# Neighbourhood attention over column blocks: 256 of the 512 grid keys for each tile of queries, keys written group by group

## What is computed

```python
NA_HEADS, HEAD_DIM, NA_WIN_R, NA_WIN_C, GRID_W = 4, 64, 8, 16, 64     # the grid has 8 rows, so a window has all of them
col_start = np.clip(cols - NA_WIN_C // 2, 0, GRID_W - NA_WIN_C)
col_idx = col_start[:, None] + np.arange(NA_WIN_C)
def row_block(r):
    rs = jnp.clip(r - NA_WIN_R // 2, 0, rows - wr)                    # always 0
    k_w = lax.dynamic_slice_in_dim(kg, rs, wr, axis=1)[:, :, col_idx]
    bias = rpb[:, dr][:, :, dc].transpose(0, 2, 1, 3)                 # by distance in rows and in columns
    s_loc = jnp.einsum('bchd,brcjhd->bhcrj', q_r, k_w) * NA_SCALE + bias
    s_ctx = jnp.einsum('bchd,bkhd->bhck', q_r, k_ctx) * NA_SCALE
    p = jax.nn.softmax(jnp.concatenate([s_loc, s_ctx]), axis=-1)
    return einsum(p_loc, v_w) + einsum(p_ctx, v_ctx)
```

## Time and profile before

| | us |
|---|---|
| median of 3 runs | 2218.65 (2218.54 to 2220.48) |
| the profiled execution: its own time | 2219.67 |
| its span in the trace | 2217.9 |
| busy: PE | 2083.6 (94%) |
| DVE | 1200.8 (54%) |
| ACT | 750.8 (34%) |
| POOL | 644.7 (29%) |

### The profile page before, as it was taken

The page is one execution under the profiler, slowest core; times in us unless marked ns, Lnnn a source line. Parts: engine busy times, 40 slices in busy tenths (PEclk is TensorE's granted clock), DMA queues, the critical chain, the costliest instruction groups (busy, mean ns, idle before and its releaser), DMA issues.

```text
span 2217.9 us, 30035 instructions
## 1 busy us (share of the span) xinstructions
PE 2083.6 (94%) x11738; PEld 1720.0 (78%) x11738; DVE 1200.8 (54%) x2143; ACT 750.8 (34%) x1221; POOL 644.7 (29%) x820
## 2 busy tenths in 40 slices
PE   7888999989989999999999998889998979999999
PEld 4777788866668888888888877778866657888887
DVE  7467524477884776177537566663368864212111
ACT  4333323456663211111111233423266643222222
POOL 1210301220002333333333430141221014555555
PEclk9999999999999999999999999999899999999999
DMA  7301431110002233233323310021110002333223
GB/s 290 105 17 34 142 107 67 39 48 10 10 10 67 76 124 124 77 114 124 105 95 114 96 52 18 20 69 39 39 48 20 10 10 77 99 100 95 95 95 105
DMA packets 76242, 165.58 MB, mean 75 GB/s; under 512 B 5192, under 2 KB 46664, under 8 KB 75088
## 3 DMA queue, kind: packets, MB, share of 16 engines
q1 hardware_dynamic: 75728, 163.28, 22.0%
q10 hardware_dynamic: 384, 0.47, 0.1%
HBM read 161.63 MB, written 2.10 MB: 74 GB/s over the span
## 4 chain that ended last, share of the span: by engine, by line
PE 79%; DVE 11%; ACT 4%; issue 4%; PEld 1%; POOL 1%; DMA 0%; PEldq 0%; DVEq 0%; SPq 0%; ACTq 0%; POOLq 0%
PE psum L1099 22%; PE psum L1100 21%; PE psum L1101 21%; PE psum L1698 1%; DVE naptlo L2107 1%; PE psum L1150 1%; PE psum L1728 1%; PE psum L1338 1%; POOL wlo L541 1%; PE psum L1467 1%; PE psum L1453 1%; PE psum L1404 1%; PE psum L1191 1%; PE psum L1223 1%; PE psum L1405 1%
## 5 line engine op out<-in xcount | busy, mean ns | idle before, releaser
L541 POOL TENSOR_TENSOR wlo<-raw,whi 128x256 fp32r<-128x256 f32 x816 | 644.5, 821 | 1564.9 <-ACT whi L566 1564.9
L1099 PE MATMUL psum<-hhi,whi 128*128 128x512 f32 (+1 forms) x1640 | 588.4, 359 | 16.8 <-DVEq L1901 8.6
L1100 PE MATMUL psum<-hlo,whi 128*128 128x512 f32 (+1 forms) x1640 | 578.9, 353 | 0.0
L1101 PE MATMUL psum<-hhi,wlo 128*128 128x512 f32 (+1 forms) x1640 | 578.2, 353 | 0.0
L566 ACT ACTIVATE whi<-raw 128x1024 fp32r<-128x1024 f32 x204 | 215.7, 1059 | 876.7 <-PE psum L1101 870.6
L1099 PEld LDWEIGHTS psum<-hhi,whi 128*128 128x128 f32 x1640 | 312.6, 191 | 73.1 <-issue 18.8
L1101 PEld LDWEIGHTS psum<-hhi,wlo 128*128 128x128 f32 x1640 | 312.2, 190 | 42.8
L1100 PEld LDWEIGHTS psum<-hlo,whi 128*128 128x128 f32 x1640 | 312.8, 191 | 40.2 <-issue 0.2
L2540 DVE TENSOR_TENSOR ffuf<-ffsa,psum 128x768 f32<-128x768 f32 (+1 forms) x44 | 36.1, 821 | 312.6 <-ACT ffsa L1049 305.9
L2525 DVE SCALAR_TENSOR_TENSOR ffmacc<-wm,csil,ffmacc 128x256 f32<-128x256 f32 x336 | 188.5, 602 | 10.4 <-DVE ffmacc L2525 5.3
L1099 PE MATMUL psum<-uhi,whi 128*128 128x512 f32 (+1 forms) x528 | 188.4, 357 | 3.7 <-DVE ulo L2544 2.1
(11 more groups left out here) (331 smaller groups left out, 3392.5 us busy)
## 6 DMA issues: line engine op xcount, KB each, us to landing
raw<-w_stream SPq DMA_DIRECT2D x204, 512.0 KB, 3.7
wm<-w_mod SPq DMA_DIRECT2D x80, 512.0 KB, 4.0
wm<-w_mod SPq DMA_DIRECT2D x8, 1024.0 KB, 12.6
xres<-x_t SPq DMA_DIRECT2D x8, 384.0 KB, 6.4
out<-xres SPq DMA_DIRECT2D x8, 256.0 KB, 2.2
consts<-c_f SPq DMA_DIRECT2D x1, 353.0 KB, 3.1
narpb<-rpb ACTq DMA_DIRECT2D x2, 120.0 KB
mlmask<-c_gate ACTq DMA_DIRECT2D x2, 108.0 KB
```

The source lines that it names most:

```text
L541: nc.gpsimd.tensor_tensor(wlo[:, q % 2, c:c + UW // 4], raw[:, q % RAW, c:c + UW // 4], whi[:, q % 2, c:c + UW // 4], ALU.subtract).then_i ...
L1099: mm(dst, ah, bh, start=first, stop=False)
L1100: mm(dst, ah, bl, start=False, stop=False)
L1101: return mm(dst, al, bh, start=False, stop=last)
```

## The change

- **Fewer keys.** The grid is cut into four query tiles of 16 columns by 8 rows (`NA_QC`) and eight key groups of 8 columns. A tile needs four neighbouring groups (`NA_G0`): 256 keys. Grid steps have 512 keys in place of 768, scores fit one PSUM bank of three, transposes go to banks 3 and 4 in turn.
- **Layout.** `key_order` writes the keys group by group, so that the 256 keys of a tile are one contiguous run; `query_order` writes the queries tile by tile. The values come out feature-major (grid 512 and context 256 columns moving), ACT copies them in group order to `navt`, PE transposes them (nine tiles, `NA_VAT`, three of them halfway between the others), then `navhi` and `navlo` as before.
- **Bias.** Three `na_bias` quads for each layer in place of 16 groups: each 32 matmuls of 32 output partitions by 128 columns, four side by side. `bias_out` copies them to `nag`; `bias_windows` makes three masked windows for each head (`nabias`), with masks that a new DMA on ACT's queue brings.
- **Softmax.** Bias, negation and minimum are one operation over 512 columns, context included (against a zero table). One exponential. The inverse row sum is applied by ACT (`scale_of`, in place), so `nadg`, the matmul with ones and the multiplication in `o_of` go.
- **Order.** Both heads of a pair alternate (a). On PE: turn(n), scores(n+2), half of the values. On DVE: max(n+1), inverse(n), `o_of`(n-5), `lo_of`(n-1). On ACT: exponential(n), copy(n-1), scale(n). Steps are as many as before: 12 for a pair in layer 0 (4 context, 8 grid), 8 in layer 1.

```diff
@@ att_plan, layout
+        def query_order(x, e):
+            return x[:, CTX_LEN:].rearrange("p (t m c e) -> p e m t c", t=4, m=4, c=16, e=2)[:, e]
+        def key_order(x):
+            return x[:, CTX_LEN:].rearrange("p (g r c) -> p r g c", g=8, c=8)
@@ PE: na_bias, values
-                for half in (0, 64):
-                    ins = mm(bias_bank(l, g)[half:half + 64, 0:240], band[:, 60 - 4 * g:60 - 4 * g + 64],
-                             NA["rb"][:, :], start=True, stop=True)
+                for g in range(4):
+                    at = 1 + 2 * (44 - 4 * (4 * q + g))
+                    for odd in range(2):
+                        for m in range(4):
+                            r = NA_WIN_R - 1 - 2 * m - odd
+                            ins = mm(bias_bank(l, q)[32 * m:32 * m + 32, P * g:P * g + P], band[:, at - odd:at - odd + 32],
+                                     rows[:, :, r:r + NA_WIN_R], start=odd == 0, stop=odd == 1)
-                    for t in range(TT):
-                        dst = bank(t)[:, 0:256]
-                        mm(dst, hhi[:, k, P * t:P * t + P], wh[:, c:c + 256], start=k == 0, stop=False)
...
+                    for f in range(2):
+                        a = slice(c + P * f, c + P * f + P)
+                        mm3(bank(f), wh[:, a], wl[:, a], hhi[:, k, CTX_LEN:], hlo[:, k, CTX_LEN:], k == 0, k == KT - 1)
...
+                    for n in {3: (0, 1), 4: (2,), 6: (3, 4)}.get(g, ()):
+                        turn_values(n)
@@ PE: att_pe
+                    if s >= 3:
+                        pe.wait_ge(s_nmx, s - 2)
...
-                for n in range(N + 3):
-                    if n < N:
-                        scores(*steps[n])
-                    if 1 <= n < N + 1:
-                        turn(*steps[n - 1])
...
+                scores(*steps[0])
+                scores(*steps[1])
+                for n in range(N + 2):
+                    if n < N:
+                        turn(*steps[n])
+                    if n + 2 < N:
+                        scores(*steps[n + 2])
+                    if n >= 2:
+                        values(n % 2, *steps[n - 1 - n % 2])
@@ ACT: att_act
+                def scale_of(s, b, kind, t, a):
+                    act.wait_ge(s_rs, s + 1)
+                    A(p, p, ACT.Copy, scale=stat[:, s % 2, 6:7]).then_inc(s_sc, 1)
...
-                    if n:
-                        hi_of(*steps[n - 1])
-                    exp_of(*st)
+                    exp_of(*st)
+                    if n:
+                        hi_of(*steps[n - 1])
+                    scale_of(*st)
@@ DVE: att_dve
+                        V.tensor_tensor_reduce(two(NA["s2"][:, s % 2, :]), two(bank(s % 3)), NA["bias"][:, 0:w + 1:w, :],
+                                               -1.0, -NEG, ALU.add, ALU.min, lowest).then_inc(s_nmx, 1)
...
+                    V.reciprocal(stat[:, s % 2, 6:7], stat[:, s % 2, 4:5]).then_inc(s_rs, 1)
...
+                max_of(*steps[0])
+                for n in range(N + 5):
+                    if n + 1 < N:
+                        max_of(*steps[n + 1])
                     if n < N:
-                        max_of(*steps[n])
...
+                        rs_of(*steps[n])
+                    if n >= 5:
+                        o_of(*steps[n - 5])
                     if 1 <= n < N + 1:
-                        rs_of(*steps[n - 1])
                         lo_of(*steps[n - 1])
```

More of the change, by code:

```diff
@@ L25 @@
 NEG = -1.0e30
+NA_X = 3
+NA_QC, NA_G0, NA_VAR = (0, 16, 32, 48), (0, 1, 3, 4), (0, 1, 1, 2)
+NA_VX = ((2, 3), (6, 7), (7, 8), (4, 5))
+NA_TILES = TT + NA_X
+NA_VAT = tuple(P * t for t in range(TT)) + tuple(CTX_LEN + 64 + P * t for t in range(NA_X))
+BIAS_QUADS = 3
+MASKS_AT = 3 * P + 122 + 2
 UW = 1024
@@ L283, in att_blocks @@
         def att_blocks(l):
-            return ([0] if l < DEPTH - 1 else []) + [1, 2]
+            return ([("c", 0), ("c", 1)] if l < DEPTH - 1 else []) + [("x", t) for t in range(4)]
         def att_plan():
@@ L717, in hi_of @@
-                def hi_of(s, b, blk, qt, nk):
+                    A(NA["p"][:, s % 3, 0:nk], NA["s2"][:, s % 2, 0:nk], ACT.Exp, bias=st[:, 0:1], scale=-1.0,
+                      accum_out=st[:, 4:5]).then_inc(s_exp, 1)
+                def scale_of(s, b, kind, t, a):
+                    nk = 256 if kind == "c" else 512
+                    act.wait_ge(s_rs, s + 1)
+                    p = NA["p"][:, s % 3, 0:nk]
+                    A(p, p, ACT.Copy, scale=stat[:, s % 2, 6:7]).then_inc(s_sc, 1)
@@ new lines, in att_pe, with scores, turn, values @@
+            def att_pe(l, pr):
+                steps = PLAN[l, pr]
+                def scores(s, b, kind, t, a):
+                    if s >= 3:
+                        pe.wait_ge(s_nmx, s - 2)
+                    dst = bank(s % 3)
+                    qh, ql = (queries(NA[x][:, a, :], kind, t) for x in ("qhi", "qlo"))
+                    ins = mm3(dst[:, 0:CTX_LEN], qh, ql, NA["khi"][:, 0:CTX_LEN], NA["klo"][:, 0:CTX_LEN], True, True)
+                    if kind == "x":
+                        at = CTX_LEN + 64 * NA_G0[t]
+                        kh, kl = (NA[x][:, at:at + 256] for x in ("khi", "klo"))
+                        ins = mm3(dst[:, CTX_LEN:512], qh, ql, kh, kl, True, True)
+                    ins.then_inc(s_ps, 1)
+                def turn(s, b, kind, t, a):
+                    pe.wait_ge(s_sc, s + 1)
+                    if s >= 2:
+                        pe.wait_ge(pt_lo, s - 1)
+                    for k in range(2 if kind == "c" else 4):
+                        ins = nc.tensor.transpose(bank(3 + s % 2)[:, P * k:P * k + P], NA["p"][:, s % 3, P * k:P * k + P], ident)
+                    ins.then_inc(t_ps, 1)
+                def values(part, s, b, kind, t, a):
+                    tiles = (0, 1) if kind == "c" else (0, 1) + NA_VX[t]
+                    half = len(tiles) // 2
@@ L2023, in query_split @@
             def query_split(l, full, a):
-                q0 = 0 if full else CTX_LEN
-                seq(split(NA["qhi"][:, a, q0:], NA["qlo"][:, a, q0:], NA["t"][:, q0:]))
+                hi_, lo_, t = NA["qhi"][:, a, :], NA["qlo"][:, a, :], NA["t"]
+                parts = [(query_order(hi_, e), query_order(lo_, e), grid_order(t, e)) for e in range(2)]
+                if full:
+                    parts.append((hi_[:, 0:CTX_LEN], lo_[:, 0:CTX_LEN], t[:, 0:CTX_LEN]))
+                for h, _, x in parts:
+                    ins = V.tensor_copy(h, x)
+                seq(ins)
+                for h, w, x in parts:
+                    ins = V.tensor_tensor(w, x, h, ALU.subtract)
+                seq(ins)
             def na_key(l, pr):
@@ L2054, in na_inputs @@
-                    if l:
-                        bias_out(l, g)
+                    if l and g in (0, 2, 5):
+                        for x in range(2):
+                            bias_out(l, (0, 2, 5).index(g), x)
+                    for n in {3: (0, 1), 4: (2,), 6: (3, 4)}.get(g, ()):
+                        values_lo(l, n)
+                    if g == 7:
+                        bias_windows(l)
                     if g == 14:
@@ L2128, in att_dve @@
                         lo_of(*steps[n - 1])
-                    if n >= 4 and steps[n - 4][4] == 1:
-                        o_of(*steps[n - 4])
+                dve.wait_ge(o_lo, steps[-1][0] + 1)
             def ml_dve(l, full):
```

349 lines of the change are left out of this document (174 added, 175 removed).

## The result

| | before | changed |
|---|---|---|
| median of five runs each, side by side | 2218.65 us (2217.44 to 2221.18) | 2208.66 us (2206.89 to 2212.73) |
| ratio, 95% interval | | 0.995 (0.9935 to 0.9965) |
| profiled execution, span | 2217.9 us | 2205.6 us |
| mean granted TensorE clock | 0.982 | 0.968 |

The changed kernel is faster by 10.0 us (0.5%), where 22.6 were forecast; 2208.66 lies outside the range of 2186 to 2207.

What follows compares the result with a forecast made beforehand. DVE paced the old attention steps; afterwards a wait through ACT, PE and DVE would. Terms -1.6, -19.7, +1.4, -4.1, +0.95 sum to -23.1 us: forecast 2196 us, range 2186 to 2207 (8 in 10).

Steps and rivals of the forecast that it cites:

- The clock: Rival: PE in the attentions at 1.2 GHz instead of 2.4 all through, +53 us, 2249 us; chance 5%.
- the loop: Attention grid steps: scaling, transposes, scores, minimum, inverse and four hand-overs follow in a circle, 3.06 us per step.
- the prediction's own layout: Attention pair's instructions in written order, each starting when engine and operands are ready: 36.8 us layer 0, 28.5 layer 1.
- The attentions otherwise: Four attentions, shortfall included: 37.3 us each in layer 0, 28.9 each in layer 1; 19.7 us gained.
- Start and layer 0: Start up to the first attention: bias groups leave PE's chain, DVE's sums of squares end 0.9 us later; -1.6 us net.
- weights that come late for the new, earlier time: Start, layer 0: late weight DMAs could take from the gain there; no size given.
- The quads: Layer 1 bias: 32 matmuls of 128 columns, four side by side, 2.0 us a quad, 6.0 for three.
- the third rival: Bias quads bound for each matmul, 4.0 us a quad: +6 us in layer 1, +3 in the start, 2205; chance 12%.
- Values and bias of layer 1: Layer 1, values to attention: cheaper bias, added transposes, a wait gone, keys' split +0.35; -4.1 us.
- the stretch with the splits: Between a layer's attentions (pair 1): query and key splits in more pieces, +1.4 us in layer 0, +0.95 in layer 1.
- The second rival: Strided outputs and splits cost DVE twice: 0.6 us per output piece, pairs 39.2 and 31.0 us, 2208; chance 9%.
- first rival: Attention grid steps set by engine work, 2.15 us each, 29 us more saved, 2167; chance 4%.

Runs made afterwards that it cites:

- The fill: Changed kernel plus unread bf16 matmuls where PE waits (seven per step, sixteen ahead of the first turn) and 26 more warming matmuls ahead of pair 1: 2196.24 us.
- the loop is cut: Changed kernel with one statement moved: on PE the scores of step n+2 run ahead of the turn of step n: 2164.4 us, ratio 0.9744.
- changed, second profile: The changed kernel unaltered, run once more on the same chip as a run beside it: 2207.28 us, ratio 0.9935.
- cut on PE, fill around the context steps: Changed kernel with scores ahead of the turn, plus unread matmuls in layer 0 only (before the first turn, context steps, warming ahead of pair 1): 2164.14 us.

## Why the prediction was wrong

**Which step failed: the clock.** The sum was made throughout at a clock of 1.00. The clock stood among the rivals, with a chance of 5%, on the argument that "three of four attentions have 1.00 with idle PE in each step". That argument read the clock of the kernel before as if it went with the place, and the change took work from PE just there. The text had the right numbers beside it ("PE's work falls from 80% to 68% of a step, and the loop holds 1.4 us of PE") and didn't carry them into the forecast. The rival was also drawn as all or nothing: half clock all through, +53 us and a slower kernel. What happened is a part of it, 68 us at half clock of the 150 us of attention. Priced by the prediction's own layout it comes out well: a pair all at half clock is 51.3 - 36.8 = 14.5 us longer in layer 0 and 40.4 - 28.5 = 11.9 in layer 1; 20.5 and 27.3 us are 0.40 and 0.53 of such a 51.3, 10.2 is 0.25 of 40.4, so 5.8 + 7.7 + 3.0 + 3.0 = 19.5 us, and 17.5 was measured. The fill gives the same from runs: it takes 14.6 us off the attentions and costs 1.8 in them, so the clock's part is some 16.4 of the 17.5. That case lay between two cases that were priced, and had no chance of its own. What stays open is why the kernel before kept its clock with PE waiting 1.0 us for the exponential: the runs show only that work put into PE's waits holds it here.

**The attentions otherwise: right.** With the clock held by the fill they take 37.8, 37.9, 29.8 and 29.8 us, and 1.8 us of that is the fill's own; forecast were 37.3, 37.3, 28.9 and 28.9. That the filled kernel's median, 2196.24, is also the forecast of 2196 is luck: its first attention begins 2.9 us earlier than before where 1.6 was forecast, its unchanged stretch between the layers is 3.4 us shorter than before, while the fill's own 3.2 us, 2.4 us more in the unchanged code behind the last attention and 1.0 in the attentions go the other way. The loop's length was 2.99 us against 3.06; ACT's scaling in it is 0.72 us where the earlier trace rows gave 0.63, and transposes and scores (1.37 for 1.42), minimum and inverse (0.79 for 0.85) and the hand-overs were shorter.

**Start and layer 0: better, by other steps.** The forecast had the sums of squares 0.9 us later than before; they begin 0.5 us earlier. The two cold quads took 5.71 us and not 6.9. DVE goes on at 11.86, as forecast, but it has made one more addition between its copies, so that five are left and not six. PE, and the last line from DVE, against the 17.66 and 12.29 of the earlier trace rows:

```profile
4.51 5.71 PE L1248 MATMUL psum<-narpb,consts 128*32 128x128 f32 x128 [4.51 <-DMA consts<-c_f]
17.20 2.90 PE L1295 MATMUL psum<-n_t,consts 128*128 128x512 f32 x4 [6.97 <-DVE n_t L2012]
...
32.43 1.87 PE L1202 MATMUL psum<-wm,csil 128*32 128x256 f32 x16 [3.13 <-DMA wm<-w_mod]
...
11.86 5.20 DVE L2012 TENSOR_TENSOR n_t<-n_t,n_sq 128x768 f32<-128x768 f32 x5
```

The wait of L1202 is the loss that the prediction named without a price, "weights that come late for the new, earlier time": PE waits 3.1 us for a DMA that nobody waited for before. In the eleven traces of kernels with this start the first attention begins at 91.6 to 93.7, so the term is -2.4 to -4.5 and not -1.6. The clock is in it too: up to the first attention the kernel before has 3.4 us at half clock, the eleven have 10.2 to 17.1. Which part of the term comes from which step I did not separate.

**The quads: right.** In layer 1 a quad takes 1.96 us, at the lower bound of 2.0; the third rival (4.0) is refuted. Values and bias of layer 1 gained 4.3 us against 4.1. The gap of the earlier trace rows before the queries is gone; a quad stands there, and the first query matmul follows without idle time:

```profile
1307.52 1.96 PE L1248 MATMUL psum<-narpb,consts 128*32 128x128 f32 x64
1309.41 0.50 PE L1151 MATMUL psum<-hhi,whi 128*128 128x512 f32 x1
```

**The strides: right.** The outputs that are written in pieces take 0.26 to 0.40 us, the key cast of 512 columns 0.42, and the stretch with the splits grew by 1.4 us in layer 0 as forecast (by 1.5 in layer 1, where 0.95 was). The second rival, with 0.6 us for an output piece, is refuted. (Its attentions of 39.2 and 31.0 add up to 9.8 us more, not 9.)

**Work sets the step (first rival): not in this kernel.** It does as soon as the loop is cut, at 1.95 us; the rival's 2167 is near what that kernel runs at, 2164. Which engine it is the prediction had wrong: it gave ACT 1.8 us and PE 2.07, and ACT has 1.95 and PE some 1.88.

## What to carry to other kernels

A change that takes work from the other engines makes TensorE wait more in the same stretch, and a waiting TensorE may be granted half its clock; where a loop runs through it, price each of its steps at both clocks, and give the mixed case a chance of its own. Before counting engine work, look for a chain that passes through every engine once per step: which instruction stands ahead of which in a hand-written order decides it, and moving one statement can be worth more than the change itself. If TensorE must wait, unread matmuls in the gap can hold the clock for little (here 3.2 us of cost against 16.4 of gain); if it has no gap, they are only work.

## What the runs showed of the hardware

**The clock without a pause.** The clock fell in an attention with no single long pause. PE's first two turns in the changed kernel, and its waits before them, the longest in this attention ahead of the fall:

```profile
95.26 0.44 PE L1407 MATMUL psum<-consts,nap 128*128 128x128 f32 x2 [1.77 <-ACT nap L766]
...
97.20 0.54 PE L1407 MATMUL psum<-consts,nap 128*128 128x128 f32 x2 [1.14 <-ACT nap L766]
```

A fill of 0.7 us in each step held it in all eight attentions in which it was tried.

**Transposes.** Six unread fp32 transposes in each step held the clock at 1.00 as seven bf16 matmuls of the same 0.7 us did.

**Unchanged code.** It varies from one execution to the next by several microseconds, and the clock goes with it. From the second attention to the values of layer 1 all kernels run the same instructions, and in four of the twelve profiles:

| kernel | at half clock in it | length |
|---|---|---|
| changed | 20.5 us | 1083.3 us |
| before | 34.1 us | 1088.0 us |
| changed, second profile | 47.8 us | 1093.8 us |
| cut on PE, fill around the context steps | 54.6 us | 1095.0 us |

The other eight lie between, at 23.9 to 34.1 us and 1084.7 to 1089.6. That is 0.34 us of time for each microsecond at half clock from the first row to the last, and it alone moves a span by 12 us. A difference between two profiles is to be taken stretch by stretch; over the whole span these 12 us can hide or fake an effect as large as the one studied. Why the low time differs between executions of the same instructions stays open.

**ScalarE.** Its four operations of a grid step overlap in the records: 0.71, 0.71, 0.19 and 0.60 us are 2.21 us added up, and the four take 1.95 from scaling to scaling.

**Pieces.** PE read a moving operand in pieces of 32 bytes, 256 bytes apart, as fast as a contiguous one: one 128x256 matmul every 0.12 us.
